# Block one's opening by channel halves: order of panels, sums and first projections in a two-block transformer kernel

## What is computed

```python
mod = c @ w_ada[l] + b_ada[l]
shift, scl, gate = jnp.split(mod, 3, axis=-1)
h = rms_norm(x, g_norm[l]) * (1.0 + scl[:, None, :]) + shift[:, None, :]
proj = h @ w_in[l]
u_pool, z_pool, q, k, v, z_attn, m_pool, m_attn = jnp.split(proj, splits, axis=-1)
```

## Time and profile before

| what | us |
|---|---|
| median of three runs | 1271.92 (1267.44 to 1272.11) |
| profiled execution | 1268.93 |
| its span, first to last instruction | 1267.1 |
| TensorE busy | 1193.6 |
| VectorE busy | 904.5 |
| ScalarE busy | 619.4 |
| GpSimd busy | 551.6 |

### The profile page before, as it was taken

The page is one execution under the profiler, slowest core; times in us unless marked ns, Lnnn a source line. Parts: engine busy times, 40 slices in busy tenths (PEclk is TensorE's granted clock), DMA queues, the critical chain, the costliest instruction groups (busy, mean ns, idle before and its releaser), DMA issues.

```text
span 1267.1 us, 19098 instructions
## 1 busy us (share of the span) xinstructions
PE 1193.6 (94%) x7186; PEld 1050.7 (83%) x7186; DVE 904.5 (71%) x1847; ACT 619.4 (49%) x1077; POOL 551.6 (44%) x323
## 2 busy tenths in 40 slices
PE   4899998899968899999999999999999999999996
PEld 2778876686747699999999999999888888888885
DVE  5678657676685643999948999999566656656566
ACT  2454444444533434444456666555445545444543
POOL 0968759474531202888877777766300000000000
PEclk9899999999978999999999999999999999999998
DMA  9988664354231431565544545455566666666664
GB/s 374 417 329 323 265 266 169 133 206 154 113 150 67 199 133 49 182 184 182 185 160 160 161 156 165 152 153 152 164 231 206 209 231 218 197 185 196 190 196 149
DMA packets 54523, 244.28 MB, mean 193 GB/s; under 512 B 6944, under 2 KB 7328, under 8 KB 42016
## 3 DMA queue, kind: packets, MB, share of 16 engines
q1 hardware_dynamic: 54000, 242.34, 55.4%
q10 hardware_dynamic: 432, 0.72, 0.2%
HBM read 240.94 MB, written 2.10 MB: 192 GB/s over the span
## 4 chain that ended last, share of the span: by engine, by line
PE 75%; DVE 4%; issue 1%; ACT 1%; POOL 0%; POOLq 0%; DVEq 0%; ACTq 0%
PE bank L1526 10%; PE bank L1523 10%; PE bank L1522 10%; PE banks L1562 5%; PE bank L1565 5%; PE bank L1568 5%; PE banks L1565 5%; PE bank L1562 5%; PE banks L1568 5%; PE banks L1536 3%; PE banks L1123 1%; PE banks L1129 1%; PE banks L1135 1%; PE banks L1393 1%; PE banks L1481 1%
## 5 line engine op out<-in xcount | busy, mean ns | idle before, releaser
L765 POOL TENSOR_TENSOR split_r<-ring,split_r 128x1024 fp32r<-128x1024 f32 x128 | 308.0, 2407 | 158.0 <-ACT split_r L996 157.9
L996 ACT ACTIVATE split_r<-ring 128x1024 fp32r<-128x1024 f32 x256 | 269.1, 1052 | 180.2 <-PE bank L1526 180.2
L1522 PE MATMUL bank<-h_high_r,split_r 128*128 128x256 f32 x1024 | 251.3, 283 | 1.7 <-ACT split_r L996 1.7
L1523 PE MATMUL bank<-h_low_r,split_r 128*128 128x256 f32 x1024 | 251.2, 283 | 0.0
L2147 DVE TENSOR_TENSOR split_r<-ring,split_r 128x1024 fp32r<-128x1024 f32 x128 | 156.8, 1225 | 65.6 <-ACT split_r L996 65.6
L1522 PEld LDWEIGHTS bank<-h_high_r,split_r 128*128 128x128 f32 x1024 | 196.3, 192 | 1.9 <-issue 1.9
L1523 PEld LDWEIGHTS bank<-h_low_r,split_r 128*128 128x128 f32 x1024 | 196.4, 192 | 0.0
L740 POOL TENSOR_TENSOR wq_low_r<-G,G_r 128x512 fp32r<-128x512 f32 (+1 forms) x104 | 135.2, 1336 | 68.5 <-ACT G_r L814 68.5
L769 POOL TENSOR_TENSOR small<-small 128x1 f32<-128x1 f32 x2 | 1.5, 760 | 359.0 <-DVE small L2173 359.0
L1526 PE MATMUL bank<-h_high_r,split_r 128*128 128x256 f32 x1024 | 143.7, 283 | 0.2 <-POOL split_r L765 0.2
L1050 ACT ACTIVATE gs_r<-G 128x256 fp32r<-128x256 f32 x128 | 53.5, 418 | 172.5 <-PE bank L1568 172.5
(11 more groups left out here) (453 smaller groups left out, 2242.1 us busy)
## 6 DMA issues: line engine op xcount, KB each, us to landing
ring<-in_down SPq DMA_DIRECT2D x128, 512.0 KB, 3.5
ring<-in_up SPq DMA_DIRECT2D x128, 512.0 KB, 3.5
G<-in_ada SPq DMA_DIRECT2D x32, 1024.0 KB, 10.5
G<-in_in SPq DMA_DIRECT2D x32, 1024.0 KB, 7.0
G<-in_out SPq DMA_DIRECT2D x8, 1024.0 KB, 8.1
G<-in_wq SPq DMA_DIRECT2D x8, 1024.0 KB, 7.7
tab<-in_ada SPq DMA_DIRECT2D x4, 1024.0 KB, 5.8
G<-in_poolup SPq DMA_DIRECT2D x2, 1024.0 KB, 6.1
```

The lines of the kernel that those rows point to most:

```text
L765: pool.tensor_tensor(wsplit[:, j % SPLIT, 1, :], raw[:, j % RAW, :], wsplit[:, j % SPLIT, 0, :].bitcast(F32), ALU.subtract).then_inc(low_r ...
L996: nc.scalar.activation(wsplit[:, n % SPLIT, 0, :], raw[:, n % RAW, :], ACT.Copy).then_inc(high_ready, 1)
L1522: mm(o, w[0][:, c, :], h_high[:, c, :], start=(c == 0), stop=False)
L1523: mm(o, w[0][:, c, :], h_low[:, c, :], start=False, stop=False)
```

## The change

The opening is cut by channel halves. The two panels for channels 0 to 511 (`ada1` 2 and 0) are summed on VectorE first; `ada1` 3 is the row; `ada1` 1 is loaded after the first halves of `in1` 2 and 3 and summed after the first half of x has been scaled and split (step `mods`). x's second half gets banks 4 and 5 and waits for its own scale and shift. TensorE does in1 2's first half, then the columns for the second half of channels, then in1 3's first half, in1 2's second and in1 3's second. From there on each projection panel is loaded ahead of the modulation panel it was behind. `LOADS` is the order of the half panels. The gates have their own semaphore and are loaded after in1 5. The `ahead` rule looks three panels ahead before in1 1 and four from it on. Line numbers of the changed kernel are larger: 1665 became 1683, 1099 became 1104, 1123 became 1128.

```diff
-STREAM += [("ada1", 2, PANEL, "dve"), ("ada1", 3, PANEL, "dve"), ("ada1", 0, PANEL, "row"), ("ada1", 1, PANEL, "dve")]
-STREAM += [("in1", 2, PANEL, "pe"), ("in1", 3, PANEL, "pe")]
-for a, b in ((("ada1", 4), ("in1", 4)), (("ada1", 5), ("in1", 5)), (("ada2", 2), ("in1", 0)), (("ada2", 3), ("in1", 1)),
-             (("ada2", 0), ("in1", 6)), (("ada2", 1), ("in1", 7)), (("ada2", 8), ("in1", 8)), (("ada2", 9), ("in1", 9))):
-    STREAM += [(*a, PANEL, "dve"), (*b, PANEL, "pe")]
+STREAM += [("ada1", 2, PANEL, "dve"), ("ada1", 0, PANEL, "dve"), ("ada1", 3, PANEL, "row"), ("in1", 2, PANEL, "pe"),
+           ("in1", 3, PANEL, "pe"), ("ada1", 1, PANEL, "dve")]
+for a, b in ((("in1", 4), ("ada1", 4)), (("in1", 5), ("ada1", 5)), (("in1", 0), ("ada2", 2)), (("in1", 1), ("ada2", 3)),
+             (("in1", 6), ("ada2", 0)), (("in1", 7), ("ada2", 1)), (("in1", 8), ("ada2", 8)), (("in1", 9), ("ada2", 9))):
+    STREAM += [(*a, PANEL, "pe"), (*b, PANEL, "dve")]
...
+LOADS = [(0, 0), (0, 1), (1, 0), (1, 1), (2, 0), (2, 1), (3, 0), (4, 0), (5, 0), (5, 1), (3, 1), (4, 1)]
+LOADS += [(n, half) for n in range(6, len(STREAM)) for half in range(2)]
...
+UNITS[1:3] = UNITS[2:0:-1]
...
-    ada_after(AT[("in1", 2)], ada)
-    high("in1", 2, (0,))
-    out.extend(("xT", 0, t, half) for t in range(NT) for half in range(2))
-    high("in1", 2, (1,))
-    panel("in1", 2)
+    ada_after(AT[("in1", 4)], ada)
+    out.extend([("xT", 0, 0, 0), ("xT", 0, 1, 0), ("high", 0), ("xsplit", 0), ("row",), ("high", 1), ("high", 2), ("mods",),
+                ("xT", 0, 0, 1), ("xT", 0, 1, 1), ("xsplit", 1), ("high", 3), ("proj", "in1", 2, 0), ("proj", "in1", 2, 1)])
...
+        elif s[0:2] == ("xT", 0) and s[3] == 1:
+            bank = 4 + s[2]
...
-            for n, (name, i, cols, user) in enumerate(STREAM):
-                if n >= SLOTS:
+            for n, half in LOADS:
+                name, i, cols, _ = STREAM[n]
+                if n >= SLOTS and half == 0:
                     panel_used(sp, n - SLOTS)
                 src = d[name] if i is None else d[name][i]
...
-                if n == SLOTS:
+                if (n, half) == (4, 1):
                     sp.dma_start(tab[:, 0:n_tab], d["tab"]).then_inc(tables_in, 16)
-                    sp.dma_start(gateA, d["gate1"].partition_broadcast(P)).then_inc(tables_in, 16)
-                    sp.dma_start(gateB, d["gate3"].partition_broadcast(P)).then_inc(tables_in, 16)
...
+                if (n, half) == (2 * SLOTS, 1):
+                    sp.dma_start(gateA, d["gate1"].partition_broadcast(P)).then_inc(gates_in, 16)
+                    sp.dma_start(gateB, d["gate3"].partition_broadcast(P)).then_inc(gates_in, 16)
+                    sp.dma_start(gfin, d["gfin1"].partition_broadcast(P)).then_inc(gates_in, 16)
...
+                elif kind == "row":
+                    act.wait_ge(row_full, 1)
+                    nc.scalar.activation(row, ps[6][0:1, :], ACT.Copy).then_inc(row_copied, 1)
+                elif kind == "xsplit":
+                    for q in range(NT):
+                        x0_high_part(q, s[1])
...
-                    if half == 0:
-                        act.wait_ge(mod_ready, blk_n + 1)
+                    act.wait_ge(mod_ready, half + 1)
...
+            for half in range(2):
+                for t in range(NT):
                     pe_.wait_ge(xn_ready, t + 1)
-                transposes(("xT", 0, t, half), [xn[0][:, t, (4 * half + c) * P:(4 * half + c + 1) * P] for c in range(4)])
+                    transposes(("xT", 0, t, half), [xn[0][:, t, (4 * half + c) * P:(4 * half + c + 1) * P] for c in range(4)])
+            make_row(0)
             start_columns(1)
-            make_row()
-            row_columns()
-            start_columns(2)
+            make_row(1)
+
...
+            def in1_products(i, halves, fill):
+
+                steps_ = [("proj", "in1", i, t) for t in range(NT)]
+                outs = [(bank_to_fill(pe_, step) if fill else ps[USE[step][0]], slice(t * P, (t + 1) * P), step)
+                        for t, step in enumerate(steps_)]
+                for half in halves:
+
+                    def x_ready(low):
+                        pe_.wait_ge(x0_low_ready if low else x0_high_ready, 1 + half if low else 2 + 2 * half)
+
+                    products(UNIT[AT["in1", i], half], [(o[:, :], tok, step) for o, tok, step in outs],
+                             x0_high, x0_low, 4 * half, x_ready)
+
+            in1_products(2, (0,), True)
+            row_columns()
+            start_columns(2)
+            in1_products(3, (0,), True)
+            in1_products(2, (1,), False)
+            in1_products(3, (1,), False)
+
...
+            def start_shift(half, src):
+
+                c4 = slice(4 * half, 4 * half + 4)
+                link(tt(modB[:, 0, c4], src[:, 0:4], b1c[:, c4], ALU.add))
+                dve.sem_inc(mod_ready, 1)
...
-            for k in range(2):
-                start_scale(k)
-            next_acc()
-            dve.wait_ge(row_cols, 1)
-            tt(modB[:, 0, 0:4], ps[7][:, 0:4], b1c[:, 0:4], ALU.add)
-            dve.wait_ge(start_cols, 3)
-            link(tt(modB[:, 0, 4:8], ps[6][:, 0:4], b1c[:, 4:8], ALU.add))
-            dve.sem_inc(mod_ready, 1)
+            dve.wait_ge(start_cols, 1)
+            start_scale(0, ps[2])
+            dve.wait_ge(start_cols, 2)
+            start_shift(0, ps[3])
...
+                elif kind == "mods":
+                    next_acc()
+                    dve.wait_ge(row_cols, 1)
+                    start_scale(1, ps[7])
+                    dve.wait_ge(start_cols, 3)
+                    start_shift(1, ps[6])
+                elif kind == "xsplit":
+                    half = s[1]
+                    dve.wait_ge(x0_high_ready, 2 + 2 * half)
+                    for t in range(NT):
+                        evacuated(dve, ("xT", 0, t, half))
+                    c = slice(4 * half, 4 * half + 4)
...
-                    ahead = [a for a in ada_steps[:-2] if a[1] < AT[(s[1], s[2])] + 3]
+                    ahead = [a for a in ada_steps[:-2] if a[1] < AT[(s[1], s[2])] + (3 if AT[(s[1], s[2])] < AT["in1", 1] else 4)]
```

More of the change, by code:

```diff
@@ L230 @@
     if s[0] in ("pv", "cmpO", "retO", "var", "norm", "y", "o", "gn", "gate", "blk", "sum", "xlow", "xout", "high", "low", "gate_load", "twice",
-                "cmpN", "rn", "rest", "query_low") or s in USE:
+                "cmpN", "rn", "rest", "query_low", "mods", "row", "xsplit") or s in USE:
         continue
@@ L672, in _ @@
                      (gcol, d["g"]), (pe, d["pe"]), (cb1, d["cb1"])]
-            for n, (name, i, cols, user) in enumerate(STREAM):
-                if n >= SLOTS:
+            for n, half in LOADS:
+                name, i, cols, _ = STREAM[n]
+                if n >= SLOTS and half == 0:
                     panel_used(sp, n - SLOTS)
                 src = d[name] if i is None else d[name][i]
-                for half in range(2):
-                    part = slice(half * (cols // 2), (half + 1) * (cols // 2))
-                    sp.dma_start(slot[n % SLOTS][:, part], src[:, part]).then_inc(panel_in[n % SLOTS][half], 16)
-                if n == 0:
+                part = slice(half * (cols // 2), (half + 1) * (cols // 2))
+                sp.dma_start(slot[n % SLOTS][:, part], src[:, part]).then_inc(panel_in[n % SLOTS][half], 16)
+                if (n, half) == (0, 1):
                     sp.dma_start(xv, d["x"]).then_inc(x_in, 16)
@@ L855, in _ @@
                     bank_free(ins, s)
-                    for q in range(NT):
-                        x0_high_part(q, half)
                 elif kind == "high":
@@ L1077, in project, with make_row @@
                 bank_full(ins, s)
-            def make_row():
-                w = slot[ROWS[0] % SLOTS].rearrange("p (c n) -> p c n", c=C)
-                for half in range(2):
-                    wait_panel(pe_, ROWS[0], (half,))
-                    for c in range(4 * half, 4 * half + 4):
-                        ins = mm(ps[6][0:1, :], c1[:, c:c + 1], w[:, c, :], start=(c == 0), stop=(c == C - 1))
-                ins.then_inc(row_full, 1)
+            def make_row(half):
+                w = wait_panel(pe_, ROWS[0], (half,)).rearrange("p (c n) -> p c n", c=C)
+                for c in range(4 * half, 4 * half + 4):
+                    ins = mm(ps[6][0:1, :], c1[:, c:c + 1], w[:, c, :], start=(c == 0), stop=(c == C - 1))
+                if half == 1:
+                    ins.then_inc(row_full, 1)
             def row_columns():
@@ L1098, in start_columns @@
                 for c in range(4):
-                    ins = mm(ps[4 + k][:, c:c + 1], acc[k % 2][:, c * P:(c + 1) * P], ones[:, 0:1], start=True, stop=True)
+                    ins = mm(ps[(2, 3, 6)[k]][:, c:c + 1], acc[k % 2][:, c * P:(c + 1) * P], ones[:, 0:1], start=True, stop=True)
                 ins.then_inc(start_cols, 1)
@@ L1104, in _ @@
             start_columns(0)
```

(23 more changed lines are left out.)

33 lines of the change are left out of this document (12 added, 21 removed).

## The result

The changed kernel takes 1306.03 us (median, 1304.87 to 1307.46) against 1270.62 us beside it, a ratio of 1.029 with a 95% interval of 1.0271 to 1.031: 35 us slower, where the prediction had 1277.5 and at most 1282. The profiled execution takes 1305.25 us with a span of 1303.4, 36.3 more than before. TensorE is busy for 1210.3 us against 1193.6, with the same number of instructions: some 17 us went into slower matmuls, the rest into waits.

What follows compares the result with a forecast made beforehand. The prediction took TensorE, busy for 94% of the span, as the bound, with time lost only where it waits. Opening +3.4 and double sum +2.2 made +5.6 us on 1271.92, so 1277.5 us; range 1266 to 1282.

Steps and rivals of the forecast that it cites:

- The opening, +3.4: Up to in1 4's start: dense work 5.7 us earlier, but in1 4 at 64.2 instead of 60.85, net +3.4 us.
- The first unit: TensorE's first dense unit in the opening: 8.2 us as before, with a cold clock at first, from 30.0 to 38.2.
- The clock behind the gap: After TensorE idles for the third sum in the opening: half speed for 3.1 to 5.6 us, taken as 2.2 us.
- No slowing under GpSimd: Rival: the opening's third sum stays at 6.0 us, no idle gap, in1 4 4.1 us earlier; 1270.0 us, chance 0.2.
- Strict exclusion: Rival: third sum's steps alternate wholly with GpSimd's pieces, 15.6 us, total +8.1, 1280.0 us; chance 0.05, within the 0.33.
- Loads cost nothing: Behind the opening: the load queue runs dry for some ten us, yet in1 5 lands before TensorE needs it; 0 us.
- The double sum, 2.2: Beside in1 1 VectorE does two sums instead of one, so TensorE waits 2.2 us for a bank ahead of in1 6.
- the clock would hold: At the 2.2 us gap ahead of in1 6: a possible clock fall, another 1.6 us, was left out of the sum.
- Then it has caught up: After in1 6: VectorE is some 2 us behind one round later, frees in1 7's banks just in time; no further loss.
- Everything at its dearest: Rival: opening's clock +0.6, clock fall ahead of in1 6 +1.6, in1 7 0.4; total 8.2, 1280.1 us, chance 0.33.

## Why the prediction was wrong

*The opening, +3.4: right, with a little luck.* The steps that set the time came where they were forecast: dense work at 29.59, a sum of 13.2 us, the gap, half clock, in1 4 0.45 us later than said; +3.5 at head 3. The first unit did not. Its 8.2 us were taken over from the kernel before, where eight matmuls took 3.75 us at half clock; here they took 2.09, and the granted clock is full:

```profile
30.00:32.00 2.00, 2.00 (x11) 1.00 0.99 414
```

That cost nothing, because the sum ended later than this unit in either case. The clock behind the gap cost more than the 2.2 us of the forecast, about 3.2 (0.7 in the columns, which took 1.73 us up to the next matmul, and 2.5 in the unit behind them, 45.82 to 53.77 against 5.44), while the sum ended 0.6 us early. "No slowing under GpSimd" (0.20) is refuted, and that the second SBUF operand is the reason is shown by the run with PSUM. One wait was missed: the third part of the first unit stood 1.64 us for GpSimd, ahead of the gap that came anyway.

*Strict exclusion: not in the long sum, but in the small operations.* The seven steps took 1.67 us each, as in the earlier trace rows, not the 2.04 of strict alternation. In the late stall each small operation did wait for the end of a piece. The Trainium skill, SBUF — State Buffer, "Who interferes with whom", says that a VectorE instruction with at most one SBUF input outside its two-port modes doesn't contend with GpSimd, and that one with two SBUF inputs does. The trace agrees: 0.79 us a step with the partial result in PSUM against 1.67. I had drawn on that section only for the price of the sum. Its condition, the second SBUF input, is also the cure, which gave 8.1 us at head 0.

*Loads cost nothing: right.* The run with only the rule undone has the new loads and loses nothing up to head 7.

*The double sum, 2.2: mis-sized in its own round.* The stall was 4.64 and the clock took another 2.5. Of the difference, 1.7 us lie between the mask and the sum: it took 110.69 - 105.94 = 4.75 us, where 3.04 was counted from the earlier trace rows. The two operations of L1744 took 2.53 us beside GpSimd's pieces; in the kernel before they came between two of its units and took 0.55:

```profile
106.10 0.55 DVE L1724 TENSOR_SCALAR ring<-ring,small 128x128 f32<-128x128 f32 x2
```

Another 0.87 is the wait between the two sums. That the clock would hold, since TensorE is dense on both sides of the gap, was the other error; the rows for a gap of 2.60 us said otherwise.

*"Then it has caught up": the step that failed.* VectorE had work for some 10 of 13 us in a round (6.3 for the sum and 3.0 for mask and norm, and small things), so by its work alone it had caught up, and the trace of before shows no wait between sums. But the sum's start also hangs on the columns of the sum two before, and the change moved the one against the other: `ada_after` puts the columns one panel later, as the modulation panels now lag, and `+ 4` keeps the sums where they were. The wait was free before because the columns were made behind the panel ahead of the sum's, 5.4 us before it began; one place further they are made behind the sum's own panel, in every round. I priced the rule by the work that it moves and not by the waits of the instructions that it moves. The first stall and the three behind it by the rule, and a fifth by the sum beside in1 9, whose columns the new pair order moved, made 33.7 us instead of 2.2; all of them but the first were put at nothing. "Everything at its dearest" had no term for a loss that comes back each round, so even the range was off by 24 us.

## What to carry to other kernels

When a step is moved earlier in an in-order queue, list all that its first instruction waits for, buffers that are written again among it, and ask for each when it is fulfilled in the new order; a wait that costs nothing in the old trace says only that it had slack. A loss in a loop of rounds is multiplied, and the clock can add to each: here stalls of 3.60 to 4.65 us cost half as much again. And where a wait protects only the last write of a chain, put it ahead of that write: this alone gave back some 21 to 23 us here.

## What the runs showed of the hardware

- Operations of 128x4 on VectorE, 0.17 us alone, took up to 1.19 beside GpSimd's subtractions of 1.24 us and ended with its pieces in the one stall where this was worked out, even a TENSOR_SCALAR with one tensor operand; TENSOR_REDUCE (0.29, 0.41) and operations that read PSUM were not slowed.
- Each of five stalls between 3.6 and 4.65 us brought the granted clock to half until 3.6 to 7.8 us after work resumed, which cost 2.5 us a time on the mean. The wait of 1.18 us at head 7 in the kernel before did not: its granted clock stays 1.00 in the slices around it.

```profile
176.00:178.00 2.00, 0.82 (x8) 0.58 (x7) 1.67 (x7) 0.84 (x4) 0.00 (x0) 1.00 1.01 422
178.00:180.00 2.00, 1.37 (x11) 1.22 (x11) 1.79 (x5) 2.00 (x5) 0.00 (x0) 1.00 1.00 422
```

- An engine that is early can lose by it: GpSimd, tied to a load, kept its time while the rest came 5 us sooner, and where nobody was slowed before, VectorE's operations now met GpSimd's pieces. What stays open is how much of the 4.7 us lead a different place for GpSimd's pieces would keep; it wasn't tried.
